# Four of sixteen attention output tiles made in halves beside the last turns of a recurrent scan

## The reference, cut to what matters

```python
o_a = mla_branch(...)                 # attention, 8 heads x 64
o_b = rwkv7_branch(...)               # recurrent scan, one forward, one backward, 8 heads x 64
y_a = o_a @ w_o_l[:MLA_WIDTH]         # "outa": 512 -> 1024
y_b = o_b @ w_o_l[MLA_WIDTH:]         # "outb": 512 -> 1024
x = x + (gates[:, :, 0] * y_a + gates[:, :, 1] * y_b) @ w_merge[l]
...
def direction(...):                   # inside rwkv7_branch, once for each direction
    o = wkv7_scan(rh, heads(decay), kh, vh, -kk, b_vec, reverse)
    o = (head_group_norm(o, ln_g, ln_b) + bonus).reshape(B, S, RWKV_WIDTH)
    return o.astype(cols.dtype) * (jax.nn.sigmoid(glo) @ g2_d)
```

## Time and profile before

| | us |
|---|---|
| median of 3 runs | 3255.03 |
| lowest and highest | 3253.57, 3256.72 |
| the profiled execution: its time | 3253.55 |
| its span (first to last instruction) | 3251.3 |
| PE busy in the span | 3132.6 (96%) |
| DVE, ACT, POOL busy | 2084.1, 1343.6, 937.5 |
| mean granted PE clock | 0.988 of 2.4 GHz |

### The profile page before, as it was taken

How to read it: one execution, slowest core, us unless ns; L and a number is a source line. 1 busy time by engine, 2 the same in 40 slices (tenths; PEclk the granted TensorE clock), 3 DMA queues, 4 the chain that set the end, 5 groups by cost and what they waited for, 6 DMA issues and landing times.

```text
span 3251.3 us, 62204 instructions
## 1 busy us (share of the span) xinstructions
PE 3132.6 (96%) x26688; PEld 2561.6 (79%) x26688; DVE 2084.1 (64%) x3018; ACT 1343.6 (41%) x2442; POOL 937.5 (29%) x810
## 2 busy tenths in 40 slices
PE   8999998999999988999999999999999999999998
PEld 8678776887788777787888888878677878888887
DVE  5263465666766665856999778752555575655686
ACT  4333334555555444533433344442332343333444
POOL 1232243222222142501576640000000025666100
PEclk9999999999999999999999999999999999999999
DMA  4241245112112122552222347422002312322753
GB/s 152 68 155 52 72 158 169 56 42 64 64 45 63 54 82 71 165 191 79 94 104 97 110 159 247 158 96 93 33 27 96 131 68 101 107 101 98 268 159 117
DMA packets 128018, 346.48 MB, mean 107 GB/s; under 512 B 15792, under 2 KB 19520, under 8 KB 124928
## 3 DMA queue, kind: packets, MB, share of 16 engines
q1 hardware_dynamic: 106592, 258.09, 23.8%
q0 software_dynamic: 21152, 84.42, 7.0%
HBM read 246.51 MB, written 95.94 MB: 105 GB/s over the span
## 4 chain that ended last, share of the span: by engine, by line
PE 84%; DVE 9%; ACT 4%; issue 2%; POOL 1%; DMA 1%; SPq 0%; DVEq 0%; ACTq 0%; POOLq 0%
PE ps L378 41%; PE ps L377 39%; PE ps L381 3%; DVE AR L387 2%; DVE X L387 2%; DVE SM L398 1%; DVE W L387 1%; ACT AR L384 1%; DVE WS L387 1%; DVE HT L391 0%; ACT WS L384 0%; ACT W L2379 0%; POOL AR L387 0%; ACT X L384 0%; DVE EX L387 0%
## 5 line engine op out<-in xcount | busy, mean ns | idle before, releaser
L387 DVE TENSOR_TENSOR WS<-W,WS 128x512 fp32r<-128x512 f32 (+1 forms) x284 | 341.7, 1204 | 245.8 <-ACT WS L384 245.6
L377 PE MATMUL ps<-HH,WS 128*128 128x512 f32 x1280 | 394.2, 389 | 0.0
L377 PE MATMUL ps<-TO,WS 128*128 128x512 f32 x1440 | 345.9, 389 | 0.0
L384 ACT ACTIVATE WS<-W 128x512 fp32r<-128x512 f32 (+1 forms) x284 | 210.0, 740 | 310.4 <-PE ps L378 165.2
L377 PEld LDWEIGHTS ps<-TO,WS 128*128 128x128 f32 x1440 | 270.3, 188 | 56.1
L377 PEld LDWEIGHTS ps<-HH,WS 128*128 128x128 f32 x1280 | 240.2, 188 | 49.9
L377 PE MATMUL ps<-HL,WS 128*128 128x512 f32 x640 | 249.0, 389 | 0.0
L378 PE MATMUL ps<-HH,WS 128*128 128x512 f32 (+1 forms) x736 | 230.3, 394 | 1.2 <-ACT HH L384 1.2
L377 PE MATMUL ps<-TO 128*128 128x512 f32 x936 | 226.8, 390 | 0.2 <-DVE TO L387 0.2
L378 PE MATMUL ps<-AR 64*64 64x64 f32 (+2 forms) x5440 | 202.8, 241 | 22.6 <-ACT AR L384 11.4
L384 ACT ACTIVATE X<-ps 128x512 f32<-128x512 f32 (+1 forms) x168 | 100.5, 598 | 284.5 <-PE ps L378 129.4
(11 more groups left out here) (387 smaller groups left out, 6530.5 us busy)
## 6 DMA issues: line engine op xcount, KB each, us to landing
AR_b<-h_d SPq DMA_DIRECT2D x154, 256.0 KB, 2.9
AR<-rw_d SPq DMA_DIRECT2D x104, 256.0 KB, 4.2
W<-in_w_fg SPq DMA_DIRECT2D x44, 512.0 KB, 3.8
W<-in_w_fu SPq DMA_DIRECT2D x44, 512.0 KB, 5.1
h_d<-FST POOLq DMA_DIRECT2D x20, 1024.0 KB, 4.4
x_d<-X POOLq DMA_DIRECT2D x24, 512.0 KB, 4.5
W<-in_w_tok SPq DMA_DIRECT2D x24, 512.0 KB, 4.0
rw_d<-X POOLq DMA_DIRECT2D x40, 256.0 KB, 3.3
```

What stands on the lines that cost most here:

```text
L377: return pe.e.matmul(o, l, r, start=start, stop=stop, skip_group_check=True)
L384: return e.e.activation(o, x, ACT.Copy)
L387: return e.e.tensor_tensor(o, x, y, op)
```

## The change

Tiles i = 0 to 3 of outa (two weight tiles, now called j = 0 and 1, each with two token halves) move out of the gn stage. PE makes each in two pieces of 6 matmuls (`outa_half`, g = 0 and 1), so 8 pieces, one behind each of the second scan's last turns, in the two SIDE banks (`outa_first_pe`). Their weights are loaded once the attention has ended, into room of the first scan's memory that is free (`SC[j].spare` and `SPARE`), and are split by ACT and POOL beside the scans' earlier turns. DVE's gated multiplies of these four stand between the second scan's last operations (`first_ve`). To let them write early, features are taken in the order `AORD` = 6, 7, 0, ... whose first two have their result in room of the first scan (EX), and the first token tile's inputs `OFE` go elsewhere. SP issues the four gate tiles of these products before the weight tiles j = 2 to 5. In the gn stage 12 outa tiles remain, two behind each of the first four token tiles and one behind each of the others.

```diff
-        OFE = EX[:, 3072:4096], AR[:, 13312:14336]
+        OFE = AR[:, 12288:13312], AR[:, 13312:14336]
+        SPARE = OBL0[:, 768:1792], WL[:, 2816:3840]
+        AORD = (6, 7, 0, 1, 2, 3, 4, 5)
...
+        def wo(j):
+            if j < 2:
+                return SC[j].spare[:, 0:512], SPARE[j][:, 512:1024], SPARE[j][:, 0:512]
+            return WO[j % 4], WOH[j % 4], WOL[j % 4]
...
         def att_out_sp(sp):
...
+            for j in range(2):
+                outa_load(sp, j)
...
         def wo_first_sp(sp):
             for g in ("pe", "ve", "ae", "ge"):
                 sp.wait_ge(*end("scan0", g))
-            for n in range(4):
-                outa_load(sp, n)
+            for i in range(4):
+                outa_gate(sp, i)
+            for j in range(2, 6):
+                outa_load(sp, j)
             for t in TORD[:2]:
                 for d in range(2):
                     sp.wait_ge(*at(f"dma_o{d}", tile_of(d, t)))
                 gn_load(sp, t)
-            for i in range(4):
-                outa_gate(sp, i)
             yield
...
+        def outa_half(pe, j, h, g, b):
+            wh, wl = [v3(z, 4) for z in wo(j)[1:]]
+            pe.wait_ge(*at("ge_mix", "wl", j))
+            pe.wait_ge(*at("ge_mix", "ol", 3, 1))
+            for k in (2 * g, 2 * g + 1):
+                mm(pe, ps[:, b, :], wh[:, k, :], OAH3[:, k, half(h)], k == 0, False)
+                mm(pe, ps[:, b, :], wh[:, k, :], OAL3[:, k, half(h)], False, False)
+                x = mm(pe, ps[:, b, :], wl[:, k, :], OAH3[:, k, half(h)], False, k == 3)
+            if g:
+                x.then_inc(*pe.sig("pe_mix", "a", 2 * j + h))
+
+        def outa_first_pe(pe):
+            for i in range(4):
+                b = take(pe, "outa", i, banks=SIDE)
+                for g in range(2):
+                    outa_half(pe, i // 2, i % 2, g, b)
                     yield
...
-                for _ in range(2 if n else 4):
+                for _ in range((2, 2, 2, 2, 1, 1, 1, 1)[n]):
                     next(outa, None)
...
-        def var_first_ve(ve):
+        def first_ve(ve):
             yield
             yield
+            for g in ("pe", "ae", "ge"):
+                ve.wait_ge(*end("scan0", g))
+            gated(ve, 0)
             ve.wait_ge(*at("ve_s1", "vr", tile_of(1, TORD[0])))
...
-                if n < 4:
-                    wo_hi(ae, n + 4)
+                if n in (1, 2):
+                    wo_hi(ae, n + 5)
...
-                if 1 <= n < 5:
-                    wo_lo(ge, n + 3)
+                if n in (2, 3):
+                    wo_lo(ge, n + 4)
```

More of the change, by code:

```diff
@@ L1894, in att_out_ae @@
                     yield
+            for j in range(2):
+                wo_hi(ae, j)
+                yield
+                yield
         def att_out_ge(ge):
@@ L1905, in att_out_ge @@
                     yield
+            for j in range(2):
+                wo_lo(ge, j)
+                yield
+                yield
         def wo_first_sp(sp):
@@ L1923, in gn_load, with wo_hi, wo_lo @@
             sp.e.dma_start(VV[:, t * 512:(t + 1) * 512], rw_d[t, 2]).then_inc(*dma(f"dma_of{t}", "all"))
[L1925 to L1933, removed]
+        def wo_hi(ae, j):
+            raw, hi, _ = wo(j)
+            ae.wait_ge(*at(f"dma_wo{j % 4}", j))
+            if j >= 6:
+                ae.wait_ge(*at("pe_mix", "a", 2 * (j - 4) + 1))
+            cp(ae, hi, raw).then_inc(*ae.sig("ae_mix", "wh", j))
+        def wo_lo(ge, j):
+            raw, hi, lo = wo(j)
+            ge.wait_ge(*at("ae_mix", "wh", j))
+            tt(ge, lo, raw, hi.bitcast(F32), ALU.subtract).then_inc(*ge.sig("ge_mix", "wl", j))
         def wo_first_ae(ae):
-            for n in range(4):
+            for j in range(2, 6):
                 yield
-                wo_hi(ae, n)
+                wo_hi(ae, j)
             yield
@@ L1943, in wo_first_ge @@
         def wo_first_ge(ge):
-            for n in range(4):
+            for j in range(2, 6):
                 yield
-                wo_lo(ge, n)
+                wo_lo(ge, j)
             yield
@@ L1963, in outa_sp @@
         def outa_sp(sp):
[L1964 to L1966 removed]
+            for j in range(8):
+                if j in (2, 3):
+                    outa_load(sp, j + 4)
                 for h in range(2):
[L1968 to L1969 removed]
+                    if 2 * j + h + 4 < 16:
+                        outa_gate(sp, 2 * j + h + 4)
+                    yield
+        def outa_half(pe, j, h, g, b):
[8 more added lines that the diff above has]
+                x.then_inc(*pe.sig("pe_mix", "a", 2 * j + h))
@@ L1970, in outa_sp @@
+        def outa_first_pe(pe):
[3 more added lines that the diff above has]
+                    outa_half(pe, i // 2, i % 2, g, b)
                     yield
         def outa_pe(pe):
[L1973 to L1984, removed]
+            for i in range(4, 16):
+                b = take(pe, "outa", i)
+                for g in range(2):
+                    outa_half(pe, i // 2, i % 2, g, b)
+                yield
@@ L1986, in outa_ve, with gated @@
+        def gated(ve, i):
+            ve.wait_ge(*at("pe_mix", "a", i))
+            ve.wait_ge(*at(f"dma_gt{i % 4}", "a", i))
+            tt(ve, mix(AORD[i // 2], half(i % 2)), GT[i % 4], ps[:, bank("outa", i), :],
+               ALU.mult).then_inc(*ve.sig("ve_mix", "a", i, frees=("outa", i)))
         def outa_ve(ve):
             scans_done(ve)
[L1988 to L1995, removed]
+            for i in range(4, 16):
+                gated(ve, i)
+                yield
@@ L2099, in var_first_ve @@
                     *ve.sig("ve_mix", "var1", d))
-            for _ in range(4):
-                yield
+            yield
+            yield
+            gated(ve, 1)
+            yield
+            yield
+            gated(ve, 2)
             ve.wait_ge(*at("ae_mix", "std1"))
             ve.e.reciprocal(VRE, VRE).then_inc(*ve.sig("ve_mix", "var2"))
+            yield
+            yield
+            gated(ve, 3)
         def gn_ae(ae):
@@ L3741, in tensor_program @@
             prep_pe(pe)
-            scans(pe, scan_pe, att_turns, att_pe, nothing, nothing)
+            scans(pe, scan_pe, att_turns, att_pe, nothing, outa_first_pe)
             gn = gn_pe(pe)
@@ L3770, in vector_program @@
             prep_over(ve)
-            scans(ve, scan_ve, att_scale_ve, att_ve, nothing, var_first_ve)
+            scans(ve, scan_ve, att_scale_ve, att_ve, nothing, first_ve)
             by_turns(gn_ve(ve), outa)
@@ L3844, in sync_program @@
             gn = gn_sp(sp)
+            for _ in range(4):
+                next(outa)
             for n in range(8):
@@ L3847, in sync_program @@
                 if n >= 2:
-                    for _ in range(2 if n > 2 else 4):
+                    for _ in range(2):
                         next(outa)
```

10 lines of the change are left out of this document (5 added, 5 removed).

## The result

The changed kernel takes 3269.5 us (median of 4 runs, 3268.6 to 3271.1) against 3254.3 (4 runs) for the kernel before: a ratio of 1.0047, 95% interval 1.0035 to 1.0059. It is slower, by about half a per cent, and 6 us above the top of the range. Its profiled execution took 3268.57 us, with a span of 3266.4.

The account below looks back on a forecast made before the run. PE and DVE, both nearly full, were taken to bound the gn stage, and a chain with PE holes the second scan's last turns. +6.6 - 5.0 = +1.6 us on 3255.03 gave 3256.6, rounded to 3256.5; range 3250.5 to 3263.5.

Parts of the forecast that it names:

- The load in front of T64: Second scan's last turns: first weight tile becomes SP's fifth transfer, so T64 starts at 1282.1 instead of 1278.2, +3.9 us.
- The rival of a load that is not held: SP's queue: weight tile lands as fast as the first transfer did, T64 2.0 us earlier, 3254.6 us; chance 0.15.
- The clock in the last turns: Second scan's last turns: PE's clock is low when T64 starts and returns to full speed at about 1286.
- T0': End of the second scan's products on PE in the changed kernel: forecast at 1295.0, +6.6 us.
- The gn stage, -5.0 us: From the end of the scan's products, outb starts after 60.9 us instead of 65.5; with shorter waits just behind, -5.0 us.
- The 44.6: Gn stage: us from DVE's first to seventh `acc`, 50.4 before, less 3.4 of waits and 2.4 for four multiplies.
- weighed POOL: Gn stage: two `wo_lo` leaving POOL free DVE a little, at most 1.1 us lower; left out of the sum.
- Behind outb's start PE is without gaps, so the shift goes through to the end: Outb to the kernel's end: PE never waits there, so the summed shift of +1.6 us reaches the total time unchanged.
- Low clock to the end of the turns: Second scan's last turns: clock stays low, scan's products end +13.5 us, net +8.5, 3263.5 us; chance 0.16.
- TensorE-bound: Gn stage: TensorE alone bounds it and DVE catches up, -11.0 us, net -4.4, 3250.6 us; chance 0.14.
- The holes are filled and no load is in the way: Last turns and gn stage: TensorE-bound, load not held, -6.4 us, and high clock, another -1.9, 3246.7 us; chance 0.06.

Follow-up runs that it names:

- e3: The kernel before, with the four gate tiles issued ahead of the four weight tiles on SP's queue; no product moved; ratio 1.0012 to the kernel before.
- e4: The change, with weight and gate tiles issued turn about on SP; ratio 1.0029 to the kernel before.
- e1: The change, with the ring of eight PSUM banks moved on by four places ahead of the gn stage; 3261.4 us, ratio 1.0026 to the kernel before.
- e12: The kernel before, without POOL's second operation of each bonus (sum with the bias row; output lacks the bias); ratio 0.9987 to the kernel before.
- e5: The change with the edits of e1 and e4 together; ratio 1.0007 to the kernel before.
- e9: The change, with 28 overwritten matmuls of 0.24 us on PE in front of its three long waits for DVE's sums; ratio 1.0046 to the kernel before.
- e10: e5 with 33 overwritten matmuls of 0.24 us on PE in front of waits in five turns of the gn stage; ratio 1.0001 to the kernel before.
- e13: e11 with 13 overwritten matmuls of 0.24 us in front of the first wait for DVE's sum and two in turn 5; ratio 0.9994 to the kernel before.
- e11: e5 with two tiles made early instead of four, fourteen left in the gn stage, ring moved on by two; 3251.1 us, ratio 0.9995 to the kernel before.
- e8: e5 without POOL's second operation of each bonus (sum with the bias row; output lacks the bias); ratio 0.9985 to the kernel before.
- e6: e5 with 28 overwritten gate-sized matmuls, 0.94 us each, on PE in front of its waits for DVE's sums; 3265.7 us, ratio 1.0040 to the kernel before.
- e2: The kernel before, with its ring of eight PSUM banks moved on by four places ahead of the gn stage; no product moved; ratio 1.0029 to the kernel before.

## Why the prediction was wrong

**The load in front of T64: right.** Forecast +3.9 us by the place in SP's queue. Counted from B it is +4.3 (8.06 for 3.75), and e3 and e4 show it from both sides; that T64 stands at 1282.03 where 1282.1 was forecast is in part luck, since B came 0.5 us earlier. The rival of a load that is not held is out: the fifth transfer landed 4.64, 4.52 and 5.60 us after its issue (the change, e1, e3). The Trainium skill (DMA: Bandwidth & Descriptors, Queues, rings and completion order) would let a later transfer end before an earlier one. The weight tiles behind the gate tiles never did so here, but such a case is in e12: the last weight tile, issued at 1280.98, landed 5.6 us later, and the `o_d` transfer issued at 1281.51 landed 4.5 us later, ahead of it.

**The clock in the last turns: right, and the sum nearly.** Low at T64, back within the half microsecond from 1287.0 (forecast 1286). T0' 1295.6 for 1295.0; counted from B it is 1.1 us later than forecast, +7.7 for +6.6.

**The gn stage, -5.0 us: the step that failed first.** Forecast 60.9 us from T0' to outb's start (-4.6, the other 0.4 just behind it), measured 65.7: +0.2 for the stage instead of -4.6. By its terms: first `acc` at T0' + 10.8 (11.6 forecast); seventh 48.1 us later (44.6 forecast); outb's start 6.8 us behind that (4.7 forecast). The 44.6 rested on two terms of DVE. Its waits for PE were to go "since PE has less to do", and its operations were to keep their length, four of 0.60 us less: 57.0 us busy where it was 59.4. The table has both in the stage, with the time at 1.2 GHz (worked out from windows of 1 us). The rows from the change to e5 have the same instructions in the stage.

| kernel | at 1.2 GHz | DVE waits for PE | DVE busy | stage |
|---|---|---|---|---|
| before | 0 | 2.2 | 59.4 | 65.5 |
| the change | 13.6 | 5.3 | 57.7 | 65.7 |
| e1 | 6.8 | 2.0 | 59.4 | 64.1 |
| e4 | 3.4 | 1.1 | 59.6 | 63.5 |
| e5 | 3.4 | 1.1 | 59.8 | 63.6 |
| e9 | 3.4 | 2.1 | 59.9 | 64.7 |
| e10 | 0 | 1.3 | 57.8 | 61.8 |

In the change the first term failed: DVE's busy time is near the forecast, and its waits grew to 5.3 us. With fewer tiles PE waits longer in one piece for `acc`, its clock falls in the wait or within 1.1 us behind it, and the gate products and the next tile, which DVE needs, then take up to twice as long. I had forecast waits of 3 us on PE, and in the tail had let waits of that size lower the clock, but not here. That the waits come from the low clock is supported by e9 (3.2 us less) and by e13 against e11 (4.9 us less). In e4 and e5 the second term failed: the waits are nearly gone, and DVE is busy 2.6 to 2.8 us more than forecast, about what the stage is above 60.9. The multiplies in SBUF beside POOL are longer: `X<-X,W` means 1178 ns in e5 and 905 in the kernel before. I had weighed POOL, and only as a gain of up to 1.1 us. e8 shows that POOL is what lengthens them. In two pairs of kernels DVE's waits and its longer operations stood in for each other: 3.2 us less of the one were 2.2 more of the other in e9, 4.9 and 3.4 in e13. That a DVE which does not wait works more of its time beside POOL would explain this, but it is not shown, and two kernels do not fit it: e10 with 57.8 us busy and hardly a wait, and e6 with 59.7 us busy and 13.4 of waits. How busy time and waits hang together stays open. The differences are one execution each, and under what the ratios can tell.

**"Behind outb's start PE is without gaps, so the shift goes through to the end": the step that cost most.** It took PE's lack of waits there as a property of the work. It was one of the bank numbers: +8.0 us, half of the whole loss. That the bank numbers cause it is shown by e1 and e2. In the change as it reads, four takes that move from `banks=BANKS` to `banks=SIDE` are the whole of it, and I read that line for its room beside the scan only.

**The rivals.** Low clock to the end of the turns did not happen. TensorE-bound with a gain of 11 us was far off. "The holes are filled and no load is in the way" got its conditions in e4 (no load, full clock), but not its gain (-6.4 us, and -1.9 by the full clock), since the stage gave 2.0 us instead of 11, and the bank numbers cost 7.7. No rival had a cost behind outb, so the range could not reach 3269.

## What to carry to other kernels

When a tile is moved from one ring of buffers to another, write down which banks its successors get, down to the next stage that has its own ring, and who reads them last: here the shift cost more than the move. Where two engines are both nearly full beside a third that slows one of them, cost the stage by all three: work taken from PE came back here as waits of DVE, and where these went, as longer operations of DVE. Ask of every longer wait of TensorE (here of 2.1 us and more) what its clock does behind it. A load that is put ahead of others in one queue is paid by all who wait for those.

## What was not expected of the hardware

The clock fell in or just behind waits that were short. With waits of 2.08, 3.00 and 2.51 us in the gn stage of the change it went to 1.2 GHz, for 3.4, 6.8 and 3.4 us; in e5 a wait of 2.04 us and one of 2.19 left it at 2.4 GHz, and only that of 3.15 us lowered it. In e1 waits of 2.08 and 2.36 us lowered it, and one of 3.43 us between them did not. So the length of one wait does not decide it alone. DVE's multiplies in SBUF went from 1178 to 929 ns on the mean when POOL did 18 operations instead of 25 beside them, at the same work of their own.
